# A hybrid decoder step: three row-wise operations of the mixer move from VectorE to GpSimd in blocks two to four

## The chip, the cores and the metric

The kernel runs on one core of one Trainium2 chip. The metric is the device time of one launch in microseconds (us); the median of the runs is compared.

## The reference

One decoder layer is computed for 2048 prompt tokens and for 32 sample tokens. With `hn = rmsnorm(x)` and `z = hn @ w_in` split into zq, zf, zi, zg, zu, zv, the part that the change touches is the mixer:

```python
S_new, o = hgrn2_scan(S0, q, k, logf, v)
o = o * lax.rsqrt(jnp.mean(o * o, axis=-1, keepdims=True) + EPS) * hg_norm_g
o_hg = o * jax.nn.sigmoid(zg)
u = jax.nn.gelu(zu)
vn = layernorm(jax.nn.gelu(zv), ln_v_g, ln_v_b)     # (v - mean) * rstd * ln_v_g + ln_v_b
o_cm = chunk_gmlp(u, vn, w_s, b_s)
x = x + jnp.concatenate([o_hg, o_cm], axis=-1) @ w_out
```

Cross attention to 256 memory tokens and an MLP of width 4096 follow, then a final RMSNorm. Everything is float32.

## The kernel before

The 2048 prompt tokens are worked through in four blocks of 512 ("first", "second", "third", "last"), one after the other; each block runs the whole layer. Every engine has one instruction stream written out by hand, and the streams meet in counted semaphores. An `Event` holds how often its semaphore is raised in each block and gives the count to wait for (`at(pos, i)`). Products are float32 in three passes of a high and a low half (line 888, `gemm`). SyncE loads the weights into an eight-deep ring; in the first block they come from the inputs, and GpSimd splits each tile into high and low halves (lines 825 and 828) that are stored as pairs; blocks two to four load the stored pairs, and GpSimd has no work there.

A block's mixer runs through eight units, u = 0 to 7 (128 tokens and two heads each). Their order on each engine is the order of its stream:

- TensorE: `within_chunk(u)` (L1022) waits for `scaled_ready` of u, and in unit 4 also for the evacuation of zg, since unit 4 is the first to use the PSUM half that zg fills. Then `fill(u + 1)` runs two or three weight tiles of the zv, zg and zu products (L888), then `rows_and_state(u)` (L1046 to L1048, L1028), which waits for `ends_ready` of u + 1 and `att_ready` of u. In unit 6 the spatial product of vn follows (L1078), which waits for `vn_ready`.
- VectorE: `attention(u)` (L2054 to L2066, one input in SBUF and one in PSUM), `new_state(u - 1)` (L2076), `args(u + 2)` (L2027, seven instructions), `scaled(u + 1)` (L2035, then seven at L2040), and then a piece of other work by unit: u = 1 the statistics of vn; u = 2 mean and reciprocal deviation applied to vn (L2136); u = 3 vn times `lng_row` (L2141); u = 4 vn plus `lnb_row` (L2145); u = 5 gate times `hgg_row` (L2149), then the mean of the squares of o (L1652); u = 6 `mixed(t)`, which multiplies o, its reciprocal root and gate (L2084), and uu with the spatial product (L2166).
- ScalarE: `decays(u + 2)` (L1516 to L1519), which waits for `args_ready` of u + 2; in unit 3 then the sigmoid of zg into gate (L1574, with a table load, L1572); then `unit_out(u)` and the squares of o (L1539).

So in unit 3 the order on ScalarE is decays(5), table load, sigmoid of zg.

Of the kernel before, what the change touches and what calls it, by code (L numbers as in the profile page):

```python
# [17 lines left out]
ALU = mybir.AluOpType  # L18
AX = mybir.AxisListType

P = 128
# [5 lines left out]
TT = BT // P  # L27
HG = 512
# [16 lines left out]
BLOCKS = ("first", "second", "third", "last")  # L45
# [153 lines left out]
def program(nc, I, O):  # L199
# [3 lines left out]
    def sb(name, shape, dt=F32, stack=ctx):  # L203
        return stack.enter_context(nc.sbuf_tensor(name, shape, dt))

    def sem(name):
        return ctx.enter_context(nc.semaphore(name))

    def event(name, mem=0, block=0, last=None, step=1, prime=0, first=None):
        return Event(sem(name), mem, block, last, step, prime, first)  # L210
# [3 lines left out]
    with ctx:  # L214
# [15 lines left out]
        hgg_row = sb("hgg_row", [P, HG])  # L230
        lng_row = sb("lng_row", [P, HG])
        lnb_row = sb("lnb_row", [P, HG])
# [34 lines left out]
        with ExitStack() as z:  # L267
            bn = sb("bn", [P, 2, TT, H, P], F32, z)
            vv = sb("vv", [P, TT, HG], F32, z)
            gate = sb("gate", [P, TT, HG], F32, z)  # L270
            vn = sb("vn", [P, TT, HG], F32, z)
# [132 lines left out]
        sig_ready = event("sig_ready", 0, 1)  # L404
        logf_ready = event("logf_ready", 0, 1)
        vn_ready = event("vn_ready", 0, 1)
        args_ready = event("args_ready", 0, UNITS)
        decays_ready = event("decays_ready", 0, UNITS)
        ends_ready = event("ends_ready", 0, UNITS)
# [16 lines left out]
        act_sem, dve_sem = sem("act_chain"), sem("dve_chain")  # L426
# [51 lines left out]
        def out(pos, job):  # L478

            h, use, *_ = jobs.of[pos, job]  # L480
            return evacuated[h].sem, evacuated[h].at(pos, use)
# [4 lines left out]
        def out_of(pos, job):  # L486
            return half[jobs.of[pos, job][0]]
# [326 lines left out]
        @block.gpsimd  # L814
        def _(pool):
            pool.sem_inc(w_split.sem, RAW)
            nc.gpsimd.memset(zero[:], 0.0).then_inc(w_rounded, 1)
            pool.wait_ge(w_rounded, 1)
            def split(g, k, skipped):

                n, s = skipped * FOLD0, k % RAW
                pool.wait_ge(w_stored[k].sem, g * 16 + (n // RING * 16 + 16))
                pool.wait_ge(w_in[s].sem, g * (16 * RING // RAW) + (n // RAW * 16 + 16 * (k // RAW + 1)))
                pool.wait_ge(w_used.sem, g * RING + (W_TILES["mem"] + skipped * FOLD1 + k + 1))
                nc.gpsimd.tensor_tensor(w_hi[:, k, :], w_raw[:, s, :], zero[:].to_broadcast([P, 512]),  # L825
                                        ALU.add).then_inc(w_rounded, 1)
                pool.wait_ge(w_rounded, g * RING + (n + k + 2))
                nc.gpsimd.tensor_tensor(w_lo[:, k, :], w_raw[:, s, :], w_hi[:, k, :].bitcast(F32),  # L828
                                        ALU.subtract).then_inc(w_split.sem, 1)

            for s in range(RING):
                pool.sem_inc(w_stored[s].sem, 16)
            with pool.Fori(0, FOLD0 // RING) as g:
                for k in range(RING):
                    if k % 4 == 0:
                        pool.wait_ge(*done("mem", ("nv", 5 if k == 0 else 7)))
                    split(g, k, 0)
            with pool.Fori(0, (W_TILES["first"] - FOLD1) // RING) as g:
                for k in range(RING):
                    split(g, k, 1)  # L840


        @block.tensor
# [802 lines left out]
        def _(dve):  # L1646
            link = Links(dve_sem)
# [11 lines left out]
            def refine(pos, tag, n):  # L1659
                c = slice(stat(tag), stat(tag) + n)  # L1660
                dve.wait_ge(rstd0_ready.sem, rstd0_ready.at(pos, tag))
                nc.vector.scalar_tensor_tensor(yt[:, c], y0[:, c], -0.5, y0[:, c], ALU.mult, ALU.mult
                                               ).then_inc(dve_sem, 1)
                dve.wait_ge(dve_sem, link.next())
                nc.vector.tensor_tensor(yt[:, c], yt[:, c], var[:, c], ALU.mult).then_inc(dve_sem, 1)
                dve.wait_ge(dve_sem, link.next())
                nc.vector.scalar_tensor_tensor(rstd[:, c], yt[:, c], 1.5, y0[:, c], ALU.add, ALU.mult
                                               ).then_inc(dve_sem, 1)
                dve.wait_ge(dve_sem, link.next())
# [41 lines left out]
            pos = "mem"  # L1711
# [63 lines left out]
            for r in range(2):  # L1775
                ins = nc.vector.tensor_tensor(lbp[:, r, :], lbp[:, r, :], lbm[:], ALU.subtract)
# [243 lines left out]
            def block_vector(pos, last):  # L2020
# [72 lines left out]
                for h in range(H):  # L2093
                    for c in range(TT):
                        s = bn[:, 1, c, h, :]
                        ins = nc.vector.tensor_tensor_scan(s, ones[:], s, 0.0, ALU.mult, ALU.add)  # L2096
# [13 lines left out]
                for u in range(UNITS):  # L2110
                    dve.wait_ge(levels_done.sem, levels_done.at(pos, u))
                    attention(u)
                    if u:
                        new_state(u - 1)
                    if u + 2 < UNITS:
                        args(u + 2)
                    if u + 1 < UNITS:
                        scaled(u + 1)
                    if u == 1:

                        dve.wait_ge(*out(pos, "zv"))
                        for t in range(TT):
                            ins = nc.vector.bn_stats(stats[:, t, :], vn[:, t, :])
                        ins.then_inc(dve_sem, 1)
                        dve.wait_ge(dve_sem, link.next())
                        nc.vector.tensor_copy(yt[:, 36:37], stats[:, TT - 1, 0:1])
                        for t in range(TT):
                            ins = nc.vector.bn_aggr(mv[:, t, :], stats[:, t, :])
                        ins.then_inc(dve_sem, 1)
                        dve.wait_ge(dve_sem, link.next())  # L2130
                        nc.vector.tensor_scalar(var[:, 16:16 + TT], mv[:, :, 1], EPS, None, ALU.add
                                                ).then_inc(var_ready.sem, 1)
                    if u == 2:
                        refine(pos, "ln", TT)
                        for t in range(TT):
                            ins = nc.vector.tensor_scalar(vn[:, t, :], vn[:, t, :], mv[:, t, 0:1],  # L2136
                                                          rstd[:, 16 + t:17 + t], ALU.subtract, ALU.mult)
                        ins.then_inc(dve_sem, 1)
                        dve.wait_ge(dve_sem, link.next())
                    if u == 3:  # L2140
                        nc.vector.tensor_tensor(vn[:], vn[:], lng_row[:, None, :].to_broadcast([P, TT, HG]), ALU.mult  # L2141
                                                ).then_inc(dve_sem, 1)
                        dve.wait_ge(dve_sem, link.next())
                    if u == 4:
                        nc.vector.tensor_tensor(vn[:], vn[:], lnb_row[:, None, :].to_broadcast([P, TT, HG]), ALU.add  # L2145
                                                ).then_inc(vn_ready.sem, 1)
                    if u == 5:
                        dve.wait_ge(*out(pos, "zg"))
                        nc.vector.tensor_tensor(gate[:], gate[:], hgg_row[:, None, :].to_broadcast([P, TT, HG]),  # L2149
                                                ALU.mult)  # L2150
                    if u == UNITS - 1:
                        rest_lo(pos, "otu", a_lo[:, 4:8, :], a_hi[:, 4:8, :], out_of(pos, "otu")[:])
                    if u == 6:
                        refine(pos, "oa", 12)
                        for t in range(3):
                            mixed(t)
                    if u == 5:
                        dve.wait_ge(o_ready.sem, o_ready.at(pos, 5))
                        mean_square(pos, "oa", 12, 1.0 / P)
                    if u == 6:  # L2160
                        dve.wait_ge(*out(pos, "zu"))
                        dve.wait_ge(*done(pos, "mix"))
                        ps = out_of(pos, "mix")
                        for g in range(H):
                            c = slice(g * P, g * P + P)
                            ins = nc.vector.scalar_tensor_tensor(uu[:, :, c], ps[:, :, c], bs_col[:, g:g + 1],  # L2166
                                                                 uu[:, :, c], ALU.add, ALU.mult)
                        ins.then_inc(evacuated_of(pos, "mix"), 1)
# [152 lines left out]
```

## Time and profile before

| | |
|---|---|
| median of 3 runs | 3029.57 us (3025.86 to 3030.86) |
| the profiled execution's own time | 3029.55 us |
| its span, first to last instruction | 3027.8 us |
| TensorE busy | 2917.4 us (96%) |
| VectorE busy | 1255.0 us (41%) |
| ScalarE busy | 720.1 us (24%) |
| GpSimd busy | 494.5 us (16%), all of it before block two's mixer |
| mean granted TensorE clock | 0.985 |

Busy shares are means over the whole span; what a change in the unit loop is worth is read from that loop. The chain that ended last gives for each moment the instruction that everything later hung on. Matmuls are pipelined, and the ends of TensorE's instructions are modelled. Where a row merges several instructions ("x7"), its duration is that of the group. PE is TensorE, PEld its weight loads, DVE VectorE, ACT ScalarE, POOL GpSimd, SP SyncE. All lines are those of the kernel before.

### The profile page before, as it was taken

To read this page: it belongs to the slowest core of one execution; us is meant where nothing else is said; L and a number is where in the kernel's file an instruction comes from. 1 tells how busy PE (TensorE), PEld (TensorE's weight loads), DVE (VectorE), ACT (ScalarE), POOL (GpSimd) and SP (SyncE) were. 2 spreads that over 40 slices of the span, in tenths; PEclk is the share of its full clock that TensorE was granted. 3 is DMA by queue.
4 is the path that set the end of the run, shared out by engine and by line. 5 is a ranking of instruction groups with operands and counts; after the bars stand their busy time and mean duration, and the time that the engine had idled before them with its cause. 6 is when DMAs were issued, how large, how long until landed. Compare 5 with 4: busy or idle time off the path is not lost.

```text
span 3027.8 us, 40427 instructions
## 1 busy us (share of the span) xinstructions
PE 2917.4 (96%) x17202; PEld 2355.5 (78%) x17202; DVE 1255.0 (41%) x2067; ACT 720.1 (24%) x1016; POOL 494.5 (16%) x389
## 2 busy tenths in 40 slices
PE   7997899999999999999999999999999989999997
PEld 6776787777878878778888778787778878877786
DVE  5668533434253833322244653222325473322233
ACT  4524222201023521201133432110103342211011
POOL 0196505787840000000000000000000000000000
PEclk9998999999999999999999999999999999999999
DMA  8796556996966345756566445566767535567654
GB/s 286 283 335 211 200 187 240 353 316 232 336 238 219 128 168 180 250 202 225 195 229 228 149 154 181 196 247 227 290 224 283 181 127 187 174 223 282 237 190 135
DMA packets 207532, 675.88 MB, mean 223 GB/s; under 512 B 22720, under 2 KB 28096, under 8 KB 207360
## 3 DMA queue, kind: packets, MB, share of 16 engines
q1 hardware_dynamic: 199760, 660.58, 62.4%
q10 hardware_dynamic: 7600, 12.78, 1.1%
q8 instruction: 135, 2.21, 0.3%
q14 instruction: 37, 0.30, 0.0%
HBM read 542.80 MB, written 130.48 MB: 222 GB/s over the span
## 4 chain that ended last, share of the span: by engine, by line
PE 89%; DVE 6%; ACT 3%; DMA 1%; issue 1%; POOL 0%; DVEq 0%; SPq 0%; ACTq 0%; POOLq 0%
PE half L888 80%; PE half L896 3%; PE half L1173 2%; DVE lvl L2027 1%; PE half L1022 1%; DVE bn L2096 1%; PE half L903 1%; DVE lvl L2040 1%; PE half L1183 0%; DMA w_pairs<-stage 0%; DVE xn L1694 0%; DVE a_lo L1675 0%; PE half L1078 0%; DVE uu L2166 0%; ACT a_hi L1354 0%
## 5 line engine op out<-in xcount | busy, mean ns | idle before, releaser
L888 PE MATMUL half<-a_hi,w_ring 128*128 128x512 f32 x2560 | 825.1, 398 | 0.1
L888 PE MATMUL half<-w_ring,a_hi 128*128 128x512 f32 x2176 | 686.6, 397 | 1.1 <-issue 1.1
L888 PE MATMUL half<-w_ring,ht_hi 128*128 128x512 f32 x2048 | 637.3, 393 | 0.0
L888 PEld LDWEIGHTS half<-a_hi,w_ring 128*128 128x128 f32 x2560 | 481.7, 188 | 132.7 <-issue 15.0
L888 PE MATMUL half<-a_lo,w_ring 128*128 128x512 f32 x1280 | 506.5, 396 | 0.0
L888 PEld LDWEIGHTS half<-w_ring,a_hi 128*128 128x128 f32 x2176 | 417.2, 192 | 94.6 <-issue 1.5
L888 PE MATMUL half<-w_ring,a_lo 128*128 128x512 f32 x1088 | 440.3, 405 | 17.9 <-DVE a_lo L1675 12.9
L888 PEld LDWEIGHTS half<-w_ring,ht_hi 128*128 128x128 f32 x2048 | 385.3, 188 | 84.0
L888 PE MATMUL half<-w_ring,ht_lo 128*128 128x512 f32 x1024 | 401.7, 392 | 0.0
L2250 DVE SCALAR_TENSOR_TENSOR x<-half,rstd,x 128x512 f32<-128x512 f32 x256 | 174.4, 744 | 304.1 <-PE half L888 304.1
L825 POOL TENSOR_TENSOR w_ring<-w_raw,zero 128x512 fp32r<-128x512 f32 x192 | 238.4, 1242 | 365.6 <-PE half L903 134.6
L888 PEld LDWEIGHTS half<-a_lo,w_ring 128*128 128x128 f32 x1280 | 241.1, 188 | 56.3
L828 POOL TENSOR_TENSOR w_ring<-w_raw,w_ring 128x512 fp32r<-128x512 f32 x192 | 261.4, 1361 | 15.0
L888 PEld LDWEIGHTS half<-w_ring,a_lo 128*128 128x128 f32 x1088 | 208.5, 192 | 65.6 <-DVE a_lo L1675 11.4
L1620 ACT ACTIVATE relu<-half 128x2048 f32<-128x2048 f32 x32 | 60.3, 1883 | 730.8 <-PE half L888 730.8
L888 PEld LDWEIGHTS half<-w_ring,ht_lo 128*128 128x128 f32 x1024 | 192.7, 188 | 43.5 <-DVE qq_s L1861 0.2
L2239 DVE TENSOR_TENSOR relu<-relu,half 128x2048 f32<-128x2048 f32 x32 | 73.2, 2288 | 312.4 <-ACT relu L1620 312.3
L1354 ACT ACTIVATE a_hi<-half 128x2048 fp32r<-128x2048 f32 (+1 forms) x34 | 62.3, 1831 | 484.8 <-PE half L896 484.8
L1675 DVE TENSOR_TENSOR a_lo<-half,a_hi 128x2048 fp32r<-128x2048 f32 (+1 forms) x34 | 75.8, 2229 | 214.5 <-ACT a_hi L1354 214.5
L888 PE MATMUL half<-w_ring,b_hi 128*128 128x512 f32 x512 | 158.9, 392 | 0.0
L888 PEld LDWEIGHTS half<-w_ring,b_hi 128*128 128x128 f32 x512 | 96.2, 188 | 21.0
L888 PE MATMUL half<-w_ring,b_lo 128*128 128x512 f32 x256 | 101.3, 396 | 6.1 <-DVE b_lo L1675 6.1
(296 smaller groups left out, 2467.0 us busy)
## 6 DMA issues: line engine op xcount, KB each, us to landing
w_ring<-w_pairs SPq DMA_DIRECT2D x704, 512.0 KB, 3.3
w_pairs<-w_ring SPq DMA_DIRECT2D x192, 512.0 KB, 4.9
w_pairs<-stage SPq DMA_DIRECT2D x16, 1024.0 KB, 5.2
w_raw<-in_w_up SPq DMA_DIRECT2D x64, 256.0 KB, 4.6
w_raw<-in_w_down SPq DMA_DIRECT2D x64, 256.0 KB, 3.9
w_s<-in_w_up SPq DMA_DIRECT2D x8, 2048.0 KB, 11.1
w_s<-in_w_down SPq DMA_DIRECT2D x8, 2048.0 KB, 11.3
w_raw<-in_w_in SPq DMA_DIRECT2D x48, 256.0 KB, 4.1
```

The lines of the kernel that those rows point to most:

```text
L825: nc.gpsimd.tensor_tensor(w_hi[:, k, :], w_raw[:, s, :], zero[:].to_broadcast([P, 512]), ALU.add).then_inc(w_rounded, 1)
L828: nc.gpsimd.tensor_tensor(w_lo[:, k, :], w_raw[:, s, :], w_hi[:, k, :].bitcast(F32), ALU.subtract).then_inc(w_split.sem, 1)
L888: m = nc.tensor.matmul(ps[:, j, :], l, r, start=(i == 0 and q == 0), stop=(i == tiles_in - 1 and q == 2))
L896: m = nc.tensor.transpose(ps[:, bank0 + i // 4, (i % 4) * P:(i % 4) * P + P], t, ident[:])
L903: m = nc.tensor.matmul(out, l, r, start=(first and i == 0), stop=(last and i == 2))
L1022: m = nc.tensor.matmul(to, keys[:, own], q, start=True, stop=True)
L1173: m = nc.tensor.matmul(ps[rows, 0, :], src[:, k, :], w_s[k // 4][:, k % 4, c * 512:c * 512 + 512], start=(k < 2), stop=(k >= KD - 2))
L1354: nc.scalar.activation(dst, src, ACT.Copy, scale=scale).then_inc(hi_ready.sem, 1)
L1620: nc.scalar.activation(relu[:], out_of(pos, ("up", e))[:], ACT.Relu).then_inc(relu_ready.sem, 1)
L1675: ins = nc.vector.tensor_tensor(dst, src, hi.bitcast(F32), ALU.subtract)
L2239: nc.vector.tensor_tensor(relu[:], relu[:], out_of(pos, ("up", e))[:], ALU.mult).then_inc(sq_ready.sem, 1)
L2250: ins = nc.vector.scalar_tensor_tensor(xc, out_of(pos, ("dn", e, c))[:, t, :], rstd[:, 24 + t:25 + t], xc, ALU.mult, ALU.add)
```

## The change

In blocks two to four GpSimd runs the three 128x2048 operations that VectorE ran in units 3, 4 and 5: vn times `lng_row`, vn plus `lnb_row`, gate times `hgg_row`. They stand behind the loops of the weight split in GpSimd's stream. The first waits for VectorE's L2136 (`vn_plain`), the second for the first (`vn_scaled`), the third for the sigmoid of zg; VectorE waits for `gate_ready` in unit 6 ahead of `mixed`. The first block keeps the old order. No DMA is added or moved, and the data are the same.

```diff
--- before.py
+++ after.py
@@ -404,6 +404,9 @@
         sig_ready = event("sig_ready", 0, 1)
         logf_ready = event("logf_ready", 0, 1)
         vn_ready = event("vn_ready", 0, 1)
+        vn_plain = event("vn_plain", 0, 1, first=0)
+        vn_scaled = event("vn_scaled", 0, 1, first=0)
+        gate_ready = event("gate_ready", 0, 1, first=0)
         args_ready = event("args_ready", 0, UNITS)
         decays_ready = event("decays_ready", 0, UNITS)
         ends_ready = event("ends_ready", 0, UNITS)
@@ -838,6 +841,17 @@
             with pool.Fori(0, (W_TILES["first"] - FOLD1) // RING) as g:
                 for k in range(RING):
                     split(g, k, 1)
+            for pos in BLOCKS[1:]:
+                wide = [P, TT, HG]
+                pool.wait_ge(vn_plain.sem, vn_plain.at(pos, 0))
+                nc.gpsimd.tensor_tensor(vn[:], vn[:], lng_row[:, None, :].to_broadcast(wide), ALU.mult
+                                        ).then_inc(vn_scaled.sem, 1)
+                pool.wait_ge(vn_scaled.sem, vn_scaled.at(pos, 0))
+                nc.gpsimd.tensor_tensor(vn[:], vn[:], lnb_row[:, None, :].to_broadcast(wide), ALU.add
+                                        ).then_inc(vn_ready.sem, 1)
+                pool.wait_ge(*out(pos, "zg"))
+                nc.gpsimd.tensor_tensor(gate[:], gate[:], hgg_row[:, None, :].to_broadcast(wide), ALU.mult
+                                        ).then_inc(gate_ready.sem, 1)
 
 
         @block.tensor
@@ -2135,16 +2149,19 @@
                         for t in range(TT):
                             ins = nc.vector.tensor_scalar(vn[:, t, :], vn[:, t, :], mv[:, t, 0:1],
                                                           rstd[:, 16 + t:17 + t], ALU.subtract, ALU.mult)
-                        ins.then_inc(dve_sem, 1)
-                        dve.wait_ge(dve_sem, link.next())
-                    if u == 3:
+                        if pos == "first":
+                            ins.then_inc(dve_sem, 1)
+                            dve.wait_ge(dve_sem, link.next())
+                        else:
+                            ins.then_inc(vn_plain.sem, 1)
+                    if u == 3 and pos == "first":
                         nc.vector.tensor_tensor(vn[:], vn[:], lng_row[:, None, :].to_broadcast([P, TT, HG]), ALU.mult
                                                 ).then_inc(dve_sem, 1)
                         dve.wait_ge(dve_sem, link.next())
-                    if u == 4:
+                    if u == 4 and pos == "first":
                         nc.vector.tensor_tensor(vn[:], vn[:], lnb_row[:, None, :].to_broadcast([P, TT, HG]), ALU.add
                                                 ).then_inc(vn_ready.sem, 1)
-                    if u == 5:
+                    if u == 5 and pos == "first":
                         dve.wait_ge(*out(pos, "zg"))
                         nc.vector.tensor_tensor(gate[:], gate[:], hgg_row[:, None, :].to_broadcast([P, TT, HG]),
                                                 ALU.mult)
@@ -2152,6 +2169,8 @@
                         rest_lo(pos, "otu", a_lo[:, 4:8, :], a_hi[:, 4:8, :], out_of(pos, "otu")[:])
                     if u == 6:
                         refine(pos, "oa", 12)
+                        if pos != "first":
+                            dve.wait_ge(gate_ready.sem, gate_ready.at(pos, 0))
                         for t in range(3):
                             mixed(t)
                     if u == 5:
```

## Rows read from the trace of the kernel before

**Rows 1.** The page: busy time of TensorE, and the chain that ended last, by engine.

```profile
PE 2917.4 (96%) x17202; PEld 2355.5 (78%) x17202; DVE 1255.0 (41%) x2067; ACT 720.1 (24%) x1016; POOL 494.5 (16%) x389
...
PE 89%; DVE 6%; ACT 3%; DMA 1%; issue 1%; POOL 0%; DVEq 0%; SPq 0%; ACTq 0%; POOLq 0%
```

**Rows 2.** Waits of TensorE in the unit loop of block three (us in total, times, longest).

```profile
PE half L1022 <- ACT gate L1574: 3.6, 1, 3.6
```

**Rows 3.** The chain in order of time in units 3 and 4, block three.

```profile
1730.20 0.69 ACT ends L1516 x2
...
1734.19 1.89 ACT gate L1574
```

**Rows 4.** Timeline of VectorE, block three: start us, us, engine, line, operation.

```profile
1722.34 1.91 DVE L2136 TENSOR_SCALAR vn<-vn,mv,rstd 128x512 f32<-128x512 f32 x4
1725.43 0.15 DVE L2054 COPY yt<-ident 128x1 f32<-128x1 f32 x1 [1.17 <-PE half L1022]
...
1727.14 0.60 DVE L2076 SCALAR_TENSOR_TENSOR state<-state,e_last,added 128x128 f32<-128x128 f32 x2
1727.66 2.50 DVE L2027 TENSOR_TENSOR lvl<-bn 128x256 f32<-128x256 f32 x7
1730.09 0.68 DVE L2035 TENSOR_TENSOR ends<-ends,kq 128x512 f32<-128x512 f32 x1
...
1733.11 2.28 DVE L2141 TENSOR_TENSOR vn<-vn,lng_row 128x2048 f32<-128x2048 f32 x1
1737.66 0.15 DVE L2054 COPY yt<-ident 128x1 f32<-128x1 f32 x1 [2.27 <-PE half L1022]
...
1739.37 0.61 DVE L2076 SCALAR_TENSOR_TENSOR state<-state,e_last,added 128x128 f32<-128x128 f32 x2
...
1745.32 2.29 DVE L2145 TENSOR_TENSOR vn<-vn,lnb_row 128x2048 f32<-128x2048 f32 x1
...
1757.94 2.29 DVE L2149 TENSOR_TENSOR gate<-gate,hgg_row 128x2048 f32<-128x2048 f32 x1
1762.00 0.17 DVE L1652 TENSOR_SCALAR var<-ss 128x12 f32<-128x12 f32 x1 [1.77 <-ACT osq L1539]
```

**Rows 5.** Timeline of TensorE, block three.

```profile
1730.87 0.46 PE L1046 MATMUL half<-vv,att 128*128 128x128 f32 x2
...
1747.23 0.38 PE L1046 MATMUL half<-vv,att 128*128 128x128 f32 x2
...
1748.87 0.27 PE L1022 MATMUL half<-kq 128*32 128x32 f32 x8
```

**Rows 6.** Timeline of GpSimd, first block, the weight split.

```profile
281.00 7.99 POOL L825 TENSOR_TENSOR w_ring<-w_raw,zero 128x512 fp32r<-128x512 f32 x1 [8.96 <-PE half L888]
...
322.37 1.30 POOL L828 TENSOR_TENSOR w_ring<-w_raw,w_ring 128x512 fp32r<-128x512 f32 x1
323.63 1.09 POOL L825 TENSOR_TENSOR w_ring<-w_raw,zero 128x512 fp32r<-128x512 f32 x1
```

**Rows 7.** Timeline of VectorE, first block, against rows 6.

```profile
285.80 2.28 DVE L2141 TENSOR_TENSOR vn<-vn,lng_row 128x2048 f32<-128x2048 f32 x1
...
322.94 1.93 DVE L2076 SCALAR_TENSOR_TENSOR state<-state,e_last,added 128x128 f32<-128x128 f32 x2
```

**Rows 8.** Line L828, GpSimd's two-input form, whole run (duration ns min/median/max).

```profile
L828 POOL TENSOR_TENSOR w_ring<-w_raw,w_ring x192: 1262/1296/5339, 136.7 to 874.5; 128x512 fp32r<-128x512 f32 x192
```

**Rows 9.** Stretches of one unit each, all engines: length, busy, then granted clock.

```profile
1023.20:1034.60 11.40, 11.32 (x150) 9.38 (x151) 9.81 (x27) 5.42 (x13) 0.00 (x0) 0.85 0.29 93
1036.10:1046.00 9.90, 9.90 (x152) 8.30 (x152) 8.44 (x27) 5.59 (x13) 0.00 (x0) 1.00 0.45 154
1736.10:1747.40 11.30, 10.09 (x150) 8.16 (x151) 9.67 (x27) 5.46 (x13) 0.00 (x0) 1.00 0.29 96
2442.10:2454.40 12.30, 12.18 (x149) 10.11 (x150) 9.88 (x27) 5.46 (x13) 0.00 (x0) 0.76 0.27 87
288.90:306.00 17.10, 12.47 (x148) 10.10 (x149) 10.30 (x27) 5.35 (x13) 8.47 (x8) 0.70 1.00 393
```

## The prediction

> **What bounds the kernel now.** I read the page first: TensorE is busy 96% of the span and holds 89% of the chain that ended last, VectorE 6% [rows 1]. VectorE work is worth something only where TensorE stands still for it. So I went to the waits of TensorE in the unit loop of one block; the second, third and last block repeat each other there, so the third stands for three. The longest wait is 3.6 us, in unit 4, for the sigmoid of zg [rows 2]. The chain shows what is ahead of that sigmoid: ScalarE starts decays(5) at 1730.20 and the sigmoid at 1734.19 [rows 3]. The timeline of VectorE shows what released ScalarE: in unit 3 the attention starts at 1725.43, the two state updates at 1727.14, args(5) at 1727.66, and these end where `ends` begins, at 1730.09, 0.11 us before decays(5) [rows 4]. So TensorE's wait hangs on one stretch of VectorE, 1725.43 to 1730.09, in each block.
>
> **What is removed.** L2141, L2145 and L2149 take 2.28, 2.29 and 2.29 us [rows 4], together 6.9 us a block, 20.6 us in three. I cost this at a gain of nothing, by what stands behind each. Behind L2141 (ends 1735.39) VectorE waits 2.27 us for TensorE before unit 4; L2145 ends at 1747.61, ahead of TensorE's unit 5, which starts at 1748.87 [rows 5]; behind L2149 (ends 1760.23) VectorE waits 1.77 us for the squares of o from ScalarE [rows 4]. None is ahead of args(5). If that cover were gone, each would be worth at most its 2.3 us.
>
> **What GpSimd pays.** No GpSimd operation of 128x2048 is in the trace. The two-input form on 512 columns has a median of 1.296 us [rows 8]. VectorE takes 0.68 us for 512 columns (L2035) and 2.28 for 2048 (L2141) [rows 4]: 1.04 ns a column and 0.15 us fixed. With the same fixed part GpSimd costs (1.296 - 0.15) / 512 = 2.24 ns a column, 4.7 us for 2048. The ends are 4.2 us (four times 1.04, the median of the cheaper form, L825, whose second input is one column; its run at 323.63 takes 1.09 us [rows 6]) and 5.2 us (four times 1.30, no fixed part). I take 4.7, since the rows of the same form are nearest. As GpSimd is empty there, this time in itself costs nothing: vn would be ready near 1734 instead of 1747.6, the gate near 1747 instead of 1760.
>
> The Trainium skill (GPSIMD Engine Reference, section 3.1) gives 4.497 us for a float32 add of 2048 columns; with it the sum below would come to about 3050.
>
> **What GpSimd takes from VectorE.** In the first block both engines work at once. A pair of state updates (two SBUF inputs each) that takes 0.60 us in unit 3 of block three [rows 4] takes 1.93 us there from 322.94 [rows 7], beside GpSimd operations at 322.37 and 323.63 [rows 6]: the first of the pair gets through as the first operation ends at 323.67, the second as the next ends at 324.72, and 0.07 us later L2035 starts [rows 7]. A VectorE instruction with two SBUF inputs thus stands until the running GpSimd instruction is over, and one or two get through between two of them. The attention ahead of the pair isn't touched; it has one input in SBUF.
>
> Now unit 3 after the change. L2136 ends at 1724.25 [rows 4]; `vn_plain` lets GpSimd start at about 1724.35, while VectorE idles until 1725.43, so GpSimd surely is first. With T for one operation, the first ends at 1724.35 + T = 1729.05. The state update issued at 1727.14 stands until then. The second GpSimd operation is issued as the first ends, as the one at 323.63 is, which lasts only 0.05 us more than 1.04 for the state update that got in before it [rows 6]. I give it 0.1 us: it runs to 1724.45 + 2T = 1733.85. The next VectorE instruction stands until then. args(5) begins at 1724.52 + 2T = 1733.9 instead of 1727.66: 2T - 3.14 = 6.3 us late (5.3 at 4.2 us, 7.3 at 5.2 us).
>
> Behind args(5) in VectorE's queue is `ends` of unit 4, which `rows_and_state(3)` waits for: TensorE, that ran it at 1730.87 without a wait [rows 5], now stands until about 1737. Behind it on ScalarE are decays(5), the table load and the sigmoid, none with slack; the sigmoid ends at 1742.4 instead of 1736.1, and unit 4 starts 6.3 us late. That is on the path, three times: 18.9 us.
>
> **The third operation** starts as the sigmoid ends, 1742.5, and runs to 1747.2. The state update of unit 4 (1739.37 before [rows 4], 1745.7 now) stands 1.5 us. What it delays is `scaled(5)`, which ended where L2145 starts, at 1745.32, and TensorE's unit 5 wanted it at 1748.87 [rows 5]: slack 3.5 us, cost nothing. The wait for `gate_ready` in unit 6 comes 20 us after the gate is done; queued behind it are only `mixed` and the uu products. Cost nothing.
>
> **The clock.** TensorE's longer stand has a second price. Unit 5 of block two, with no stand ahead of it, lasts 9.9 us at full clock. Unit 4 is 11.4, 11.3 and 12.3 us in blocks two, three and last, at clocks of 0.85, 1.00 and 0.76 [rows 9]: 1.8 us a block is already paid (a part of it, in block three, as an idle gap and not as clock). In the first block, where two stands of 3.6 and 4.6 us come close together, the granted clock of the stretch is 0.70 and the busy time 12.5 us [rows 9]: 2.6 us more than unit 5. After the change two stands of about 6.1 and 4.0 us follow one another. I take 3.1 us, so 1.3 more than now, 3.9 in three blocks. The ends: nothing more than now; and half the speed (1.2 instead of 2.4 GHz) for some 10 us of the stretch, which adds 5.1, that is 3.3 more than the 1.8 paid now.
>
> **The sum.** 3 x (6.3 + 1.3) = 22.8 us on the profiled execution's own 3029.55, which is the median of the runs (3029.57) but for 0.02: **3052 us**.
>
> **The rivals.**
>
> *VectorE keeps the door.* In the first block there is another pattern: the GpSimd operation that arrives at 281.00, amid a string of VectorE instructions, lasts 7.99 us, until the string's last (285.80 and 2.28) is over [rows 6, 7]. If the second operation fares so, VectorE's delay is that of the first alone, 1729.05 + 0.33 - 1727.66 = 1.7 us, and the second slips in at about 1734.8, when VectorE waits for TensorE anyway. Then 3 x 1.7 = 5.2: 3035 us. For it: that row, one of four like it in the first block's units. Against it: all four follow a pause of GpSimd, while an operation that follows on another has been let in after one or two VectorE instructions. Here the second follows on the first. 14%.
>
> The Trainium skill (SBUF — State Buffer, "Who interferes with whom") has the loser wait for one whole instruction, by order of issue; by that alone the second operation would be let in at once, as in my forecast. The 7.99 us, through a whole string of instructions, are more than it says.
>
> *No effect.* The collisions are as in the first block but fall in time that TensorE doesn't miss, or the long operation, whose second input is one row read four times, holds VectorE less than the short ones do. Then 3029.6. Against it: the path from args(5) has 0.11 us of slack. 10%.
>
> *Faster.* If the wait for the squares of o in unit 5 is put down wrongly and L2149 delays unit 6, its removal gives up to 2.3 us a block: 3029.6 - 6.9 = 3023. It decides only if ScalarE's squares are done before 1760.23, and if GpSimd's first two operations do no harm. The 1.77 us wait speaks against it. 5%.
>
> *Beyond the range.* GpSimd's price is above 5.2 us, so that the gate's operation holds unit 4's update for more than the 3.5 us of slack too. At T = 7 this is 10.9 + 3.3 us a block: 3072. 5%.
>
> The forecast has 66%; its own range is 3045 (5.3 and nothing for the clock: 15.9) to 3061 (7.3 + 3.3: 31.8). Down to the first rival, the range is 3035 to 3061, which leaves out what is below and above, some 17%. About 0.2% (6 us) can be told from no change here. Slower by more: the forecast, the last case and the larger part of the first rival, which lies at the bound: 80%. Within: 15%. Faster: 5%.
>
> **What would show it.** In blocks two to four: GpSimd operations of 4.2 to 5.2 us at L2136's end; two state updates in unit 3 that last 6 to 7 us together instead of 0.60; args(5) 6.3 us late; a wait of TensorE for `ends` ahead of `rows_and_state(3)` and a second before unit 4; a lower granted clock in unit 4; vn and gate ready long before their use. I am wrong if the pair in unit 3 lasts 2.5 us with GpSimd's second operation stretched, or if VectorE isn't held at all.

## The result, and the profile after

| | before | after |
|---|---|---|
| median of 5 runs each | 3029.57 us (3025.86 to 3030.86) | 3047.12 us (3040.32 to 3052.23) |
| ratio of the runs | | 1.0057, interval 1.0041 to 1.0073 |
| the profiled execution: own time, span | 3029.55, 3027.8 us | 3049.91, 3048.1 us |
| mean granted TensorE clock | 0.985 | 0.981 |

The change makes the kernel 17.5 us slower by the medians, 20.4 us by the two profiled executions.

All lines below are those of the kernel that is shown. After the change those behind the diff's hunks stand 3 to 19 lower in the code (L888 is L902, L1022 is L1036, L1046 is L1060, L2027 is L2041, L2035 is L2049, L2076 is L2090, L2136 is L2150). The timeline of GpSimd after, block three; it answers to nothing in the kernel before, where GpSimd was empty here:

```profile
1731.17 4.62 POOL L847 TENSOR_TENSOR vn<-vn,lng_row 128x2048 f32<-128x2048 f32 x1 [697.61 <-DVE vn L2150]
1735.87 4.54 POOL L850 TENSOR_TENSOR vn<-vn,lnb_row 128x2048 f32<-128x2048 f32 x1
1748.95 4.57 POOL L853 TENSOR_TENSOR gate<-gate,hgg_row 128x2048 f32<-128x2048 f32 x1 [8.54 <-ACT gate L1588]
```

The three operations last 4.62, 4.54 and 4.57 us. The timeline of VectorE in the same units, to be held against [rows 4]:

```profile
1729.18 1.92 DVE L2150 TENSOR_SCALAR vn<-vn,mv,rstd 128x512 f32<-128x512 f32 x4
1732.20 0.15 DVE L2068 COPY yt<-ident 128x1 f32<-128x1 f32 x1 [1.11 <-PE half L1036]
...
1733.91 6.66 DVE L2090 SCALAR_TENSOR_TENSOR state<-state,e_last,added 128x128 f32<-128x128 f32 x2
1740.49 2.48 DVE L2041 TENSOR_TENSOR lvl<-bn 128x256 f32<-128x256 f32 x7
1742.89 0.68 DVE L2049 TENSOR_TENSOR ends<-ends,kq 128x512 f32<-128x512 f32 x1
...
1752.89 1.04 DVE L2090 SCALAR_TENSOR_TENSOR state<-state,e_last,added 128x128 f32<-128x128 f32 x2
```

L2150 ends at 1731.10 and GpSimd starts 0.07 us later. The attention starts at 1732.20 as before, 1.1 us behind, and isn't stretched. The two state updates last 6.66 us instead of 0.60: they end at 1740.57, right behind GpSimd's second operation (1735.87 + 4.54 = 1740.41), and args(5) (L2041) starts at 1740.49. In unit 4 the pair lasts 1.04 us, held by the gate's operation. The waits of TensorE in this unit loop, which answer to [rows 2]:

```profile
PE half L1060 <- issue: 5.8, 1, 5.8
...
PE half L1036 <- ACT gate L1588: 2.0, 1, 2.0
```

The wait of 3.6 us for the sigmoid has become two, 5.8 and 2.0 us. The first is ahead of L1060, `rows_and_state(3)`. The view names no releaser for it; what ends 0.1 us ahead of it is `ends` of VectorE (1742.89 + 0.68 = 1743.57). The timeline of TensorE:

```profile
1737.24 0.63 PE L902 MATMUL half<-w_ring,a_hi 128*128 128x512 f32 x2
1743.67 0.76 PE L1060 MATMUL half<-vv,att 128*128 128x128 f32 x2 [5.80 <-issue]
...
1746.36 0.63 PE L1042 MATMUL half<-ident,ends 128*128 128x128 f32 x2
1749.02 0.34 PE L1036 MATMUL half<-kq 128*32 128x32 f32 x8 [2.02 <-ACT gate L1588]
...
1761.28 0.38 PE L1060 MATMUL half<-vv,att 128*128 128x128 f32 x2
```

The product ahead ends near 1737.9; L1060 starts at 1743.67, where before it followed at once [rows 5], and lasts 0.76 us instead of 0.46, at a lower clock. `rows_and_state(3)` as a whole takes 3.3 us (1743.67 to 1746.99) where it took 1.8 (1730.87 to 1732.66), and these 1.5 us fall into the wait for the sigmoid that follows anyway. The granted clock is 0.50 from L1060 to 1747.0 and, behind the second wait, from 1749.0 to 1755.1 (1.2 of 2.4 GHz), and 1.00 from 1755.3. The stretches of unit 4 in blocks two, three and last (length, then busy times, and the granted clock after POOL's), against the 11.4, 11.3 and 12.3 us of [rows 9]:

```profile
1029.00:1041.30 12.30, 12.23 (x149) 10.18 (x150) 8.13 (x26) 5.41 (x13) 4.56 (x1) 0.76 0.27 84
1749.00:1761.30 12.30, 12.28 (x149) 10.16 (x150) 8.13 (x26) 5.36 (x13) 4.52 (x1) 0.75 0.26 86
2462.10:2474.50 12.40, 12.31 (x148) 10.23 (x149) 8.14 (x26) 5.43 (x13) 4.56 (x1) 0.74 0.26 82
```

The unit itself, from its first matmul to the next `rows_and_state`, lasts 12.1 to 12.4 us, at 0.74 to 0.76 of the clock in all three blocks; before, blocks two, three and last had 0.85, 1.00 and 0.76. Its first matmul and the next `rows_and_state` in the kernel before, blocks two, three and last (that of block three at 1747.23 is in [rows 5]):

```profile
1023.27 0.24 PE L1022 MATMUL half<-kq 128*32 128x32 f32 x5 [3.55 <-ACT gate L1574]
...
1034.46 0.38 PE L1046 MATMUL half<-vv,att 128*128 128x128 f32 x2
...
1736.22 0.24 PE L1022 MATMUL half<-kq 128*32 128x32 f32 x5 [3.56 <-ACT gate L1574]
...
2442.22 0.34 PE L1022 MATMUL half<-kq 128*32 128x32 f32 x8 [3.56 <-ACT gate L1574]
...
2454.30 0.38 PE L1046 MATMUL half<-vv,att 128*128 128x128 f32 x2
```

**A measure for the experiments.** Whole executions of one kernel differ by several us (those of the kernel before, run beside the experiments, lay between 3022.5 and 3039.5), much of it in the first block, which the change leaves alone: in kernels that are equal up to there, VectorE's `vn` operation of block two ends at 1008.2 us in one and at 1015.5 us in another. So I also use one stretch of each block: from the end of VectorE's `vn` operation in unit 2 (L2136 before) to the first matmul of the spatial product in unit 6 (L1078 before). It holds all that the change touches. In us, from the timelines; each ratio is taken against executions of the kernel before beside that kernel's own, whose medians lay between 3026.86 and 3029.57 us:

| kernel | block two | three | last | median us | ratio, interval |
|---|---|---|---|---|---|
| before | 45.2 | 45.0 | 46.1 | | |
| after | 52.1 | 52.2 | 52.3 | 3047.12 | 1.0057 (1.0041 to 1.0073) |
| dead reads (block two alone) | 51.4 | 46.1 | 45.9 | one run, 3033.04 | |
| dead writes (block two alone) | 45.0 | 46.0 | 45.9 | one run, 3032.64 | |
| old slots | 45.9 | 44.9 | 46.0 | 3028.14 | 0.9997 (0.9988 to 1.0006) |
| first operation alone | 46.5 | 46.7 | 46.7 | 3028.29 | 1.0000 (0.9991 to 1.0009) |
| gate alone | 45.1 | 45.9 | 45.0 | 3028.74 | 1.0001 (0.9992 to 1.0010) |
| sigmoid first | 45.4 | 45.6 | 45.5 | 3029.38 | 1.0002 (0.9993 to 1.0011) |
| after, sigmoid first | 51.6 | 51.9 | 52.1 | 3048.14 | 1.0063 (1.0049 to 1.0077) |
| old slots, sigmoid first | 46.4 | 45.6 | 45.5 | 3029.57 | 1.0000 (0.9990 to 1.0009) |
| sigmoid and rows first | 40.6 | 42.1 | 40.8 | 3012.78 | 0.9950 (0.9937 to 0.9962) |
| the same with old slots | 40.6 | 41.6 | 40.6 | 3012.58 | 0.9952 (0.9939 to 0.9965) |
| second operation mid-string | 51.1 | 51.4 | 50.9 | 3048.17 | 1.0067 (1.0055 to 1.0079) |
| first alone, mid-string | 43.5 | 44.9 | 46.0 | 3028.27 | 1.0002 (0.9993 to 1.0011) |

The stretches of after less those of before are 6.9, 7.2 and 6.2 us, 20.3 together: the whole difference of the two profiled executions. The blocks that the two dead runs leave as they were differ from the kernel before by up to 1.1 us, so a single stretch is not read closer than that.

### The profile page after: what moved, and what is told of

Same layout as the page of the kernel before. It is cut to its first block, busy times and chain, and to the rows that moved or that the text cites. A ratio compares the mean times of both kernels' runs of the same rounds, so it can differ in the third digit from the quotient of the medians.

```text
span 3048.1 us, 40424 instructions
## 1 busy us (share of the span) xinstructions
PE 2923.7 (96%) x17202; PEld 2360.8 (77%) x17202; DVE 1257.1 (41%) x2058; ACT 720.1 (24%) x1016; POOL 532.4 (17%) x398
## 4 chain that ended last, share of the span: by engine, by line
PE 88%; DVE 7%; ACT 3%; DMA 1%; issue 1%; POOL 0%; DVEq 0%; SPq 0%; ACTq 0%; POOLq 0%
PE half L902 79%; PE half L910 3%; PE half L1187 2%; PE half L1036 1%; DVE lvl L2041 1%; DVE state L2090 1%; DMA w_pairs<-stage 1%; DVE bn L2110 1%; DVE lvl L2054 1%; PE half L1197 0%; DVE xn L1708 0%; DVE a_lo L1689 0%; PE half L917 0%; PE half L1092 0%; DVE uu L2185 0%
## 5 line engine op out<-in xcount | busy, mean ns | idle before, releaser
L902 PE MATMUL half<-a_hi,w_ring 128*128 128x512 f32 x2560 | 824.1, 397 | 0.1
L902 PE MATMUL half<-w_ring,a_hi 128*128 128x512 f32 x2176 | 687.1, 398 | 0.0
L902 PE MATMUL half<-w_ring,ht_hi 128*128 128x512 f32 x2048 | 637.5, 393 | 0.0
L902 PEld LDWEIGHTS half<-a_hi,w_ring 128*128 128x128 f32 x2560 | 481.1, 188 | 132.6 <-issue 14.9
L902 PE MATMUL half<-a_lo,w_ring 128*128 128x512 f32 x1280 | 506.1, 395 | 0.0
L902 PEld LDWEIGHTS half<-w_ring,a_hi 128*128 128x128 f32 x2176 | 417.8, 192 | 92.9
L902 PE MATMUL half<-w_ring,a_lo 128*128 128x512 f32 x1088 | 440.9, 405 | 17.7 <-DVE a_lo L1689 13.4
L902 PEld LDWEIGHTS half<-w_ring,ht_hi 128*128 128x128 f32 x2048 | 385.4, 188 | 84.1
L902 PE MATMUL half<-w_ring,ht_lo 128*128 128x512 f32 x1024 | 401.8, 392 | 0.0
L828 POOL TENSOR_TENSOR w_ring<-w_raw,zero 128x512 fp32r<-128x512 f32 x192 | 232.7, 1212 | 370.3 <-PE half L917 133.8
L902 PEld LDWEIGHTS half<-a_lo,w_ring 128*128 128x128 f32 x1280 | 240.6, 188 | 56.2
L847 POOL TENSOR_TENSOR vn<-vn,lng_row 128x2048 f32<-128x2048 f32 x3 | 13.8, 4616 | 1522.4 <-DVE vn L2150 1522.4
L902 PEld LDWEIGHTS half<-w_ring,a_lo 128*128 128x128 f32 x1088 | 209.2, 192 | 65.9 <-DVE a_lo L1689 11.7
L902 PEld LDWEIGHTS half<-w_ring,ht_lo 128*128 128x128 f32 x1024 | 192.6, 188 | 43.5 <-DVE qq_s L1875 0.2
L902 PE MATMUL half<-w_ring,b_hi 128*128 128x512 f32 x512 | 158.7, 391 | 0.0
L902 PEld LDWEIGHTS half<-w_ring,b_hi 128*128 128x128 f32 x512 | 96.2, 188 | 21.2
## 6 DMA issues: line engine op xcount, KB each, us to landing
w_s<-in_w_up SPq DMA_DIRECT2D x8, 2048.0 KB, 12.1
w_s<-in_w_down SPq DMA_DIRECT2D x8, 2048.0 KB, 11.4
```

Source lines behind the costliest of these rows:

```text
L902: m = nc.tensor.matmul(ps[:, j, :], l, r, start=(i == 0 and q == 0), stop=(i == tiles_in - 1 and q == 2))
```

## The experiments

The theory: a VectorE instruction with two inputs in SBUF stands while a GpSimd instruction reads SBUF. Its main rival: the time is lost in handing work to another engine and waiting for it.

**Dead reads.** The kernel before, whole; in block two GpSimd also does three operations of the change's size and form on `w_raw`, which holds nothing there.

```diff
+            for i, row in enumerate((lng_row, lnb_row, hgg_row)):
+                if i == 0:
+                    pool.wait_ge(dead_go, 1)
+                if i == 2:
+                    pool.wait_ge(*out("second", "zg"))
+                nc.gpsimd.tensor_tensor(w_raw[:], w_raw[:], row[:, None, :].to_broadcast([P, TT, HG]),
+                                        ALU.add if i == 1 else ALU.mult).then_inc(dead_done, 1)
+                pool.wait_ge(dead_done, i + 1)
```

> VectorE does all its own work as in the kernel before; in block two alone GpSimd runs, at the times of the change, three operations of the same size and form on a buffer that is dead there. Theory (a VectorE instruction with two SBUF inputs stands while a GpSimd instruction that reads SBUF runs): the pair of state updates in unit 3 of block two lasts 6.7 us instead of 0.60, unit 4 of TensorE starts 6 us late, and the block is 6 to 7 us longer: span near 3034.5 against 3027.8. Rival (the time is lost in handing vn and the gate over to another engine and waiting for them): nothing is handed over, so the pair lasts 0.60 us and the span stays near 3028.

Timelines of GpSimd and of VectorE in unit 3 of block two:

```profile
1008.35 4.63 POOL L847 TENSOR_TENSOR w_raw<-w_raw,lng_row 128x2048 f32<-128x2048 f32 x1 [133.60 <-DVEq L2150]
1013.06 4.55 POOL L847 TENSOR_TENSOR w_raw<-w_raw,lnb_row 128x2048 f32<-128x2048 f32 x1
```

```profile
1011.00 6.75 DVE L2085 SCALAR_TENSOR_TENSOR state<-state,e_last,added 128x128 f32<-128x128 f32 x2
```

The waits of TensorE in block two:

```profile
PE half L1055 <- issue: 5.9, 1, 5.9
...
PE half L1031 <- ACT gate L1583: 2.0, 1, 2.0
```

The pair of state updates lasts 6.75 us and TensorE stands for 5.9 and 2.0 us as after the change (5.8 and 2.0), though VectorE needs nothing of GpSimd's (its one wait for it, in unit 6, keeps `w_raw` from being loaded anew and is long met), and the stretch is 6.2 us longer in block two; in the other two blocks it is within 1.1 us of the kernel before. The one run has a span of 3030.2, 4 us less than expected; its stretch in block two begins 3.1 us earlier than in the kernel before (1008.2 against 1011.3), ahead of anything that the edit touches. So nearly the whole loss (6.2 of the 6.9 us) is there without any handing over, and the rival falls.

**Dead writes.** The same with memsets, which write and read nothing.

```diff
+            for i in range(9):
+                ...
+                nc.gpsimd.memset(w_raw[:], 0.0).then_inc(dead_done, 1)
+                pool.wait_ge(dead_done, i + 1)
```

> As the run with dead reads, but the dead GpSimd work is nine memsets of 128x2048, which write SBUF and read nothing. Theory in its narrow form (only GpSimd's reads hold VectorE up): the pair of state updates in unit 3 of block two lasts 0.60 us and the span stays near 3028. In its wide form (any GpSimd instruction on SBUF holds VectorE up): the pair is stretched, by up to one memset for each of the two.

```profile
1015.62 11.14 POOL L847 MEMSET w_raw<- 128x2048 f32 x6 [134.27 <-DVEq L2149]
```

```profile
1018.30 0.60 DVE L2084 SCALAR_TENSOR_TENSOR state<-state,e_last,added 128x128 f32<-128x128 f32 x2
```

Six memsets run from 1015.62 to 1026.76, across the pair, args(5) and scaled(4), and none is stretched: 0.60, 2.51 and 0.68 us. A GpSimd instruction that only writes doesn't hold VectorE up; one that reads SBUF does.

**Old slots.** The kernel after; each operation also waits for VectorE's `scaled` of unit 4, 5, 6.

```diff
                 pool.wait_ge(vn_plain.sem, vn_plain.at(pos, 0))
+                pool.wait_ge(scaled_ready.sem, scaled_ready.at(pos, 4))
...
                 pool.wait_ge(vn_scaled.sem, vn_scaled.at(pos, 0))
+                pool.wait_ge(scaled_ready.sem, scaled_ready.at(pos, 5))
...
                 pool.wait_ge(*out(pos, "zg"))
+                pool.wait_ge(scaled_ready.sem, scaled_ready.at(pos, 6))
```

> The kernel after, but each GpSimd operation also waits for the end of scaled(4), scaled(5) and scaled(6), where VectorE did the same work before; there VectorE has no two-input instruction for more than 5 us. Theory: GpSimd's 4.6 us fall into VectorE's pauses and attentions, the state updates stay at 0.60 us, and the time is that of the kernel before, 3029.6 within 3 us. Rival (handing over to GpSimd costs, wherever it is): slower than before by most of the 17.5 us.

```profile
1736.13 4.53 POOL L848 TENSOR_TENSOR vn<-vn,lng_row 128x2048 f32<-128x2048 f32 x1 [683.31 <-DVE lvl L2057]
```

```profile
1729.93 0.61 DVE L2093 SCALAR_TENSOR_TENSOR state<-state,e_last,added 128x128 f32<-128x128 f32 x2
...
1742.10 0.61 DVE L2093 SCALAR_TENSOR_TENSOR state<-state,e_last,added 128x128 f32<-128x128 f32 x2
```

GpSimd's 4.53 us end at 1740.66, ahead of unit 4's pair at 1742.10, and both pairs last 0.61 us. The time is that of the kernel before. What the change hands over costs nothing; where it put it cost the 17.5 us.

**The first operation alone** (the other two back on VectorE).

```diff
-                    if u == 4 and pos == "first":
+                    if u == 4:
+                        if pos != "first":
+                            dve.wait_ge(vn_scaled.sem, vn_scaled.at(pos, 0))
```

> Only the first operation (vn times its weight) goes to GpSimd, the other two stay on VectorE. Theory: the first state update of unit 3 stands until GpSimd's one operation is over, 1731.17 + 4.62 in the time of the kernel after, so args(5) is 6.06 - 4.6 = 1.4 us late in each block; with a little for the clock 4 to 7 us in all: 3034 to 3037. Rival (the delay comes with the last operation, the gate's, or with the wait for it): 3029.6, nothing lost.

```profile
1724.51 2.32 DVE L2084 SCALAR_TENSOR_TENSOR state<-state,e_last,added 128x128 f32<-128x128 f32 x2
```

The pair lasts 2.32 us, so args(5) is 1.7 us late, as the prediction's first rival has it (the expectation above has 1.4), and the stretches are 1.3, 1.7 and 0.6 us longer, 3.6 together. The measured time doesn't show it: 1.0000, with an interval of 2.7 us to either side. I expected 4 to 7 us. The delay is shown, its effect on the end isn't.

**The gate's operation alone** (vn stays on VectorE).

```diff
-                    if u == 3 and pos == "first":
+                    if u == 3:
...
-                    if u == 4 and pos == "first":
+                    if u == 4:
```

> Only the gate's operation goes to GpSimd, in the kernel after's place (right behind the sigmoid of zg); vn stays on VectorE. Theory: it starts near 1736.1 and ends near 1740.7, so the state updates of unit 4 (1739.37) stand 1.3 us, inside the slack of 3.5 us that scaled(5) has: 3029.6 within 3 us, TensorE's unit 5 not late. Rival (the three operations share the harm): a third of the 17.5 us, 3035.

```profile
1740.52 0.97 DVE L2084 SCALAR_TENSOR_TENSOR state<-state,e_last,added 128x128 f32<-128x128 f32 x2
```

The pair of unit 4 lasts 0.97 us instead of 0.61; the time is unchanged. The third operation costs nothing, as forecast.

**The sigmoid first.** The kernel before with ScalarE's order changed in unit 3, in all four blocks.

```diff
-                    if u + 2 < UNITS:
+                    if u + 2 < UNITS and u != 3:
                         decays(u + 2)
                     for at, name, dst in ((0, "zv", vn), (3, "zg", gate), (6, "zu", uu)):
                         ...
+                    if u == 3:
+                        decays(u + 2)
```

> The kernel before with the sigmoid of zg ahead of decays(5) on ScalarE in unit 3, in all four blocks. If TensorE's unit 4 hangs on decays(5), the table load and the sigmoid, as the chain of the kernel before has it, the sigmoid is done near 1732.9 instead of 1736.1 and TensorE's 3.6 us wait goes: 3.3 us in four blocks, and up to 1.8 a block of clock: 3009 to 3017. Rival: scaled(5) or unit_out(3), now later on ScalarE by 1.3 to 2 us, becomes the next wait: 3020 to 3030.

```profile
PE half L888 <- ACT vv L1534: 3.2, 1, 3.2
```

No gain. TensorE's wait for the sigmoid is gone, and a wait of 3.2 us for `unit_out(3)` (L1534) has come in its place: `fill(5)` writes the PSUM half that it empties, and it now stands behind decays(5). The rival came in.

**After, with the sigmoid first.** The same edit on the kernel after.

> The kernel after with the sigmoid of zg first. Theory: the gate's operation is then ready to go when GpSimd's second ends, so three follow one another; VectorE gets one or two instructions in between the second and the third, and args(5) stands for a third 4.6 us. Unit 4 of TensorE starts 7 to 8 us later than in the kernel before, 1 to 2 later than in the kernel after, though its old wait for the sigmoid is gone; the first block gains 3.3: 3043 to 3052. Rival (the loss passes through decays(5) and the sigmoid alone): with the sigmoid ahead of decays(5) it goes, 3010 to 3020.

```profile
1729.31 4.62 POOL L847 TENSOR_TENSOR vn<-vn,lng_row 128x2048 f32<-128x2048 f32 x1 [705.69 <-DVE vn L2152]
1734.01 4.56 POOL L850 TENSOR_TENSOR vn<-vn,lnb_row 128x2048 f32<-128x2048 f32 x1
1738.52 4.54 POOL L853 TENSOR_TENSOR gate<-gate,hgg_row 128x2048 f32<-128x2048 f32 x1
```

```profile
1732.04 6.67 DVE L2092 SCALAR_TENSOR_TENSOR state<-state,e_last,added 128x128 f32<-128x128 f32 x2
1738.64 6.78 DVE L2043 TENSOR_TENSOR lvl<-bn 128x256 f32<-128x256 f32 x7
```

With the sigmoid done early the three operations follow one another (1729.31 to 1743.06), the state updates get in ahead of the second and of the third, and args(5), whose first instruction stands for the third, lasts 6.78 us instead of 2.50. TensorE's waits in block three:

```profile
PE half L1060 <- issue: 10.1, 1, 10.1
```

The wait for the sigmoid is gone, and all of it stands ahead of `rows_and_state(3)`, which needs the `ends` that follows args(5) (1745.34 + 0.68 = 1746.02; TensorE starts at 1746.12). The time is 3048, inside the range, and not the 3010 to 3020 of a loss that passes through decays(5) and the sigmoid alone: the delay of args(5) reaches TensorE by `ends` too.

**Old slots with the sigmoid first.**

> GpSimd's operations in VectorE's old slots and the sigmoid first. Theory: VectorE's work in these slots is off the path, so this is the time of the kernel before with the sigmoid first, within 3 us. Rival: with TensorE's wait gone VectorE is nearer to the path, and its 6.9 us a block less is worth something: faster than that by 5 us or more.

3029.57, that of the sigmoid first alone (3029.38).

**Sigmoid and rows first.** In unit 3 `unit_out(3)` goes ahead of decays(5) too, again in all four blocks.

```diff
                     unit_out(u)
+                    if u == 3:
+                        decays(u + 2)
```

> The kernel before with, in unit 3 on ScalarE, the sigmoid of zg first, then unit_out(3), then decays(5). With the sigmoid first alone TensorE waited 3.2 us in unit 4 for unit_out(3), which stood behind decays(5). Theory: with both ahead of decays(5) neither wait is left, and each block's stretch from the end of the statistics of vn to the spatial product is 3.2 to 3.6 us shorter than in the kernel before, up to 1.8 more by the clock: 3010 to 3017. Rival: decays(5), some 5 us later than before, makes scaled(5) late for TensorE's unit 5: 3018 to 3028.

```profile
PE half L888 <- DVE a_lo L1677: 2.9, 1, 2.9
...
PE half L1022 <- DVE lvl L2042: 0.6, 1, 0.6
```

Waits of TensorE in block three: neither the sigmoid nor L1534 is among them, and 0.6 us for VectorE's `scaled` is. The 2.9 us are there in the kernel before as well. The stretches are 4.6, 2.9 and 5.2 us shorter, the first block's is 3.0 us shorter, and the kernel is 0.50% faster than before (0.38 to 0.63%), 15 us. This is the version that beats both.

**The same with GpSimd in the old slots.**

> The same order on ScalarE, with GpSimd's three operations in the slots behind scaled(4), scaled(5) and scaled(6). Theory: VectorE's 6.9 us a block are off the path here too: the time of the run before this one, within 3 us. Rival: in a block that is 3.3 us shorter the slots are tighter, GpSimd's 4.6 us reach the state updates of the next unit, and it is slower than that by 3 us or more.

3012.58 against 3012.78: no difference. VectorE's 6.9 us a block are worth nothing here either, with 0.6 us of TensorE waiting for it.

**The second operation in the middle of a string.** The kernel after, with GpSimd's second operation waiting for the state updates of unit 3 too, so that it arrives while VectorE runs args(5).

```diff
                 pool.wait_ge(vn_scaled.sem, vn_scaled.at(pos, 0))
+                pool.wait_ge(added_used.sem, added_used.at(pos, 2))
```

> The kernel after, but GpSimd's second operation also waits for the two state updates of unit 3, so that it arrives 0.4 us later, when the string args(5), scaled(4) is under way. If a GpSimd operation that arrives in the middle of a string of VectorE's two-input instructions waits for the string's end (as the one of 7.99 us in the first block), args(5) isn't stretched, the second operation lasts 9 to 11 us, and only the first one's 1.7 us a block are lost: 3028 to 3035. If whoever asks first is served next, args(5) stands another 4.5 us and the time is that of the kernel after, 3045 to 3050.

```profile
1734.25 4.67 POOL L851 TENSOR_TENSOR vn<-vn,lnb_row 128x2048 f32<-128x2048 f32 x1 [0.56 <-DVE state L2091]
```

It is served at once (4.67 us against 4.54), and args(5) stands. The long wait of the first block's 7.99 us doesn't come from arriving in mid-string.

**The first operation alone, in the middle of the string.**

```diff
                 pool.wait_ge(vn_plain.sem, vn_plain.at(pos, 0))
+                pool.wait_ge(added_used.sem, added_used.at(pos, 2))
```

> Only the first operation goes to GpSimd, and it waits for the two state updates of unit 3, so that it arrives in the middle of VectorE's string args(5), scaled(4), after a pause of GpSimd of hundreds of us. In the run whose second operation arrived in the same string 0.56 us after the first, GpSimd was served after one VectorE instruction (4.66 us). Theory one (it is the pause of GpSimd that puts it behind the string, as with the 7.99 us of the first block): here the operation lasts 9 to 10.5 us, args(5) is not stretched and the time is 3026 to 3031. Theory two (an operation of this form is served after one VectorE instruction wherever it comes from; the first block's long waits belong to its form or to something else): it lasts 4.6 to 4.9 us, args(5) stands 4.5 us, TensorE's unit 4 is 4.5 us late in each block: 3038 to 3046.

```profile
1728.73 9.68 POOL L848 TENSOR_TENSOR vn<-vn,lng_row 128x2048 f32<-128x2048 f32 x1 [701.88 <-DVE state L2085]
```

```profile
1728.50 2.50 DVE L2036 TENSOR_TENSOR lvl<-bn 128x256 f32<-128x256 f32 x7
1730.91 0.69 DVE L2044 TENSOR_TENSOR ends<-ends,kq 128x512 f32<-128x512 f32 x1
1731.52 2.52 DVE L2049 TENSOR_TENSOR lvl<-lvl,kq 128x256 f32<-128x256 f32 x7
```

Here the operation lasts 9.68 us: it arrives at 1728.73, VectorE's string isn't stretched and ends at 1734.04, and GpSimd ends 4.37 us after that. Nothing is lost: 3028.27. Size and place in the string are those of the run before (0.23 and 0.22 us behind the start of args(5)); the operation is a multiply and there an add, which take 4.62 and 4.54 us when VectorE doesn't keep them out. What else differs is that there GpSimd had worked until 0.56 us before and VectorE had just stood for it. Which of these two decides is open. The pause needn't be long: in the first block of the kernel before, GpSimd operations that came into such strings after pauses of 5.24, 1.17, 8.96 and 3.38 us lasted 4.00, 5.67, 7.99 and 7.89 us instead of 1.04.

## Why the prediction was right

- **The path.** TensorE's unit 4 hangs on args(5) through decays(5) and the sigmoid. Shown by the after trace (args(5) 6.0 us late in each block, unit 4 6.0 us late) and by the sigmoid and rows first, which takes decays(5) off the path and gains 15 us. The second route that the prediction names, `ends` into `rows_and_state(3)`, carries the whole delay when the sigmoid stands ahead of decays(5) (after, sigmoid first). The two stands of TensorE were 5.8 and 2.0 us, forecast 6.1 and 4.0; the second was shorter mostly because `rows_and_state(3)`, between the two, took 1.5 us more at a lower clock.
- **Nothing gained by the removal.** Shown by the old slots: VectorE has 20.6 us less to do, and the time stays, with or without the sigmoid and rows first.
- **GpSimd's price, 4.7 us.** 4.62, 4.54 and 4.57. The Trainium skill (GPSIMD Engine Reference, section 3.1) gives 4.497 us for the add; the trace has 4.54, 1% more, and up to 3% more for the multiplies. By the prediction's own terms an estimate with the page's figure is 3051.
- **VectorE held up.** Shown to be GpSimd's reads (dead reads, dead writes). The delay 2T - 3.14 was 6.3 us; in block three the stretch from the end of L2136 to args(5) grew from 3.41 to 9.39 us, by 6.0. The term is right but for T (2 x 4.58 - 3.14 = 6.0). The runs add that a GpSimd instruction which only writes doesn't do it.
- **The third operation free.** Shown by the gate alone. Forecast was that it holds unit 4's pair for 1.5 us; after the change it was 0.4 (1.04 instead of 0.60), since unit 4's products ran at a lower clock and the pair came later.
- **The clock, 1.3 us a block more: too much.** Unit 4 lasts 12.14, 12.26 and 12.37 us (1029.07 to 1041.21, 1749.02 to 1761.28, 2462.19 to 2474.56) against 11.18, 11.01 and 12.09 (1023.27 to 1034.46, 1736.22 to 1747.23, 2442.22 to 2454.30): 2.5 us in three blocks instead of 3.9. Forecast was 3.1 us above unit 5 of block two, taken from the first block; it is 2.6 (unit 5 lasts 9.63, 1036.10 to 1045.73), and the last block was near that level before. That the lower clock follows the stands is borne out: behind the 5.8 us it is there in all three blocks, behind the 3.6 us before it was there in two of them.
- **The sum.** 3 x 6.0 + 2.5 = 20.4, which is the difference of the profiled executions (20.4 of their own times, 20.3 of their spans); forecast 22.8. Of the 2.4 us too much, 1.4 are the clock's and 1.0 the delay's (T). The medians lie 17.5 us apart, since the profiled execution of the kernel after is above its median: of the 5 us between 3052 and 3047, about half is this scatter. The chances outside the range add up to 20% and not to some 17%.
- **Who is let in.** Forecast: one or two VectorE instructions between GpSimd's operations; one was. The rival, that the second operation waits for the whole string, did not come, and the reason given against it (it follows on another) fits the cases seen: an operation was let in when it followed on another after 0.08 or 0.56 us, and kept out of a string when it came after a pause, of hundreds of us in the last run and of 1.2 to 9.0 in the first block. That the pause is the reason isn't shown: that VectorE had just stood, or not, explains the same cases. By the Trainium skill (SBUF — State Buffer, "Who interferes with whom") whoever issues first holds the shared ports for its whole instruction; that fits the former (4.54 and 4.67 us) and not the 9.68 us, which outlast fifteen instructions of VectorE.

## What to carry to other kernels

Work taken from an engine that waits anyway gives nothing, and an engine with idle time isn't free if its instructions hold up another's: ask of each GpSimd instruction of several us that reads SBUF which two-input VectorE instructions fall into it, and who waits for them. If it must go to GpSimd, tie its start to a point behind which VectorE has nothing of the kind for its length. When the first wait of a chain is moved, look at what the same engine now does later: the sigmoid alone gave nothing, the sigmoid and the rows 15 us.

## What the runs showed of the hardware that I had not expected

- A GpSimd operation of 4.6 us that arrives after a pause, while VectorE runs two-input instructions back to back, isn't done until 4.4 us behind the last of them: 9.68 us, three times alike. Right after another GpSimd operation it is served after one or two.
- A GpSimd memset of 128x2048 takes 1.8 us (11.14 us for six, each waiting for the one ahead), and VectorE's two-input instructions aren't stretched by it (a pair in 0.60 us).
- `attention`'s predicated copies, with the mask in SBUF and the data in PSUM, run beside GpSimd's reads without a stretch (1732.20 to 1733.91, 1.71 us, as before).
